# Expert rows spread over partitions by a permuted constant, and the last products among the expert turns made transposes (decoder step with mixture of experts, one core)

## The reference, cut to what matters

```python
def hmoe(h, w_rg, b_rg, w_re, b_re, w_g, w_u, w_d):
    g_prob = softmax(h @ w_rg + b_rg)              # 4 groups, the best one is taken
    e_logits = (h @ w_re + b_re)[the 8 experts of that group]
    top_p, top_i = top_k(softmax(e_logits), 2)     # two of its 8 experts
    weights = max(g_prob) * top_p / sum(top_p)
    expert = g_idx * 8 + top_i                     # 32 experts in all
    a = einsum('td,edf->tef', h, w_g)              # 1024 -> 256
    u = einsum('td,edf->tef', h, w_u)
    return einsum('tef,efd->td', silu(a) * u * comb[:, :, None], w_d)   # 256 -> 1024
```

```
layer 0: 47 40 35 37 40 27 33 39 23 31 37 25 28 21 34 27 33 33 32 32 38 26 30 34 28 36 32 27 30 40 33 32
layer 1: 25 39 35 28 33 27 25 22 32 28 31 40 28 32 32 17 34 31 44 49 27 42 37 32 23 44 37 32 36 30 35 33
```

## Time and profile before

| | |
|---|---|
| median of 3 runs | 1375.42 us |
| the profiled execution: its own time | 1374.61 us |
| its span, first to last instruction | 1372.7 us |
| PE busy | 1297.9 us, 95% of the span |
| DVE, ACT, POOL busy | 637.2, 332.1, 451.9 us |
| moved by DMA | 318.83 MB, mean 232 GB/s |
| mean granted clock of PE | 0.987 |
| mixture of layer 0, first gate product to last | 367 to 586 us |
| mixture of layer 1, the same | 1125 to 1348 us |

### The profile page before, as it was taken

One profiled execution on the slowest core, in us unless ns is written; L12 is line 12 of the kernel. 1 busy time (PEld: TensorE's weight loads), 2 busy tenths in 40 slices (PEclk: granted clock), 3 DMA queues, 4 the chain that ended last, 5 costly groups with the idle time before them and its releaser, 6 DMA issues. The chain is left out here.

```text
span 1372.7 us, 20982 instructions
## 1 busy us (share of the span) xinstructions
PE 1297.9 (95%) x8732; PEld 919.7 (67%) x8732; DVE 637.2 (46%) x997; ACT 332.1 (24%) x667; POOL 451.9 (33%) x385
## 2 busy tenths in 40 slices
PE   8999999999999998899999999999998989999786
PEld 6787888545566764547868867877845656766453
DVE  3577675623622221164558558558436472121114
ACT  2222322302122221240115005005005312222112
POOL 2233444101011111005876576576450111111101
PEclk9999999999899999999999999999999999999998
DMA  8366534377699999971112012013050899999996
GB/s 312 135 219 220 194 106 174 101 309 299 246 418 418 419 418 420 412 289 51 57 56 94 12 55 94 11 56 96 9 139 2 330 353 419 417 419 419 419 417 259
DMA packets 92768, 318.83 MB, mean 232 GB/s; under 512 B 32969, under 2 KB 45401, under 8 KB 66564
## 3 DMA queue, kind: packets, MB, share of 16 engines
q1 hardware_dynamic: 77956, 279.95, 52.5%
q0 software_dynamic: 13536, 33.29, 6.7%
q10 hardware_dynamic: 1184, 4.26, 0.8%
HBM read 300.19 MB, written 33.28 MB: 243 GB/s over the span
## 5 line engine op out<-in xcount | busy, mean ns | idle before, releaser
L1941 PE MATMUL ps<-slots 128*128 128x384 f32 x768 | 262.0, 495 | 0.9 <-DVE vo L2240 0.6
L1941 PEld LDWEIGHTS ps<-slots 128*128 128x128 f32 x768 | 203.0, 270 | 43.7 <-issue 3.2
L1092 PE MATMUL ps<-slots,oT 128*64 128x256 f32 x1344 | 178.4, 390 | 23.3 <-DMA slots<-in_w_up 18.6
L581 PE MATMUL ps<-xnT_a,wA 128*128 128x260 f32 (+1 forms) x768 | 173.3, 386 | 1.7 <-DVE xnT_a L791 1.4
L1092 PEld LDWEIGHTS ps<-slots,oT 128*64 128x64 f32 x1344 | 121.4, 141 | 74.2 <-issue 26.2
L581 PEld LDWEIGHTS ps<-xnT_a,wA 128*128 128x128 f32 x768 | 145.6, 191 | 27.0 <-issue 5.8
L1604 POOL DMA_INDIRECT y_rows<-ysb,idx x30 | 30.2, 1007 | 361.1 <-DVE ysb L1127 361.1
L1118 DVE TENSOR_TENSOR sg<-sg,ps 64x256 f32<-64x256 f32 x64 | 26.5, 414 | 236.2 <-ACT sg L1115 236.2
L1127 DVE COPY ysb<-ps 64x512 f32<-64x512 f32 x60 | 41.6, 694 | 82.8 <-PE ps L1110 82.8
L1115 ACT ACTIVATE sg<-ps 64x256 f32<-64x256 f32 x64 | 24.4, 381 | 227.5 <-PE ps L1092 227.5
L2178 ACT ACTIVATE slots<-slots,neg 128x128 f32<-128x128 f32 (+1 forms) x192 | 64.1, 417 | 54.8 <-DVE neg L2285 49.3
(11 more groups left out here) (311 smaller groups left out, 2129.5 us busy)
## 6 DMA issues: line engine op xcount, KB each, us to landing
slots<-in_w_gate SPq DMA_DIRECT2D x42, 1024.0 KB, 23.2
slots<-in_w_up SPq DMA_DIRECT2D x42, 1024.0 KB, 26.6
slots<-in_w_down SPq DMA_DIRECT2D x36, 1024.0 KB, 26.1
slots<-in_unit_weights_b SPq DMA_DIRECT2D x12, 1536.0 KB, 7.1
wA<-in_qkv_pairs_a SPq DMA_DIRECT2D x24, 512.0 KB, 4.4
apart<-in_w_down SPq DMA_DIRECT2D x8, 1024.0 KB, 27.8
spare<-in_w_down SPq DMA_DIRECT2D x8, 1024.0 KB, 24.5
apart<-in_w_up SPq DMA_DIRECT2D x6, 1024.0 KB, 27.9
```

Of the source, the lines that this page charges most:

```text
L581: last = nc.tensor.matmul(bank(6 + h)[:, 0:half], wA[:, m, k, :], xnT[:, k, half * h:half * h + half], start=(k == 0), stop=(k == KT - 1))
L1092: last = nc.tensor.matmul(bank(q)[lo:lo + CAP, 0:FE], x[:, k, :], wt[:, k, :], start=(k == 0), stop=(k == KT - 1))
L1941: last = nc.tensor.matmul(bank(i % 2)[:, 0:UW], xT[:, kt, cols], wB[:, g, kt, :], start=(kt == 0), stop=(kt == KT - 1))
```

## The change

The constant with which places are compared is permuted: slot s now belongs to place s // 4 + 16 * (s % 4). Put the other way round, row r of an expert now sits in slot 4 * (r % 16) + r // 16: rows 0 to 15 in slots 0, 4, 8, ..., 60, rows 16 to 31 in slots 1, 5, ..., 61, and so on. The constant keeps its size and the instructions that use it stay as they are. And the product that stood first in the turn of `xs`, and the first of the two of each expert in the turn of h, become transposes. The instructions stand at the same place in PE's order; on the other engines none is added, removed or moved.

```diff
-    put("iota64", np.broadcast_to(np.arange(CAP), (128, CAP)))
+    slot = np.arange(CAP)
+    put("iota64", np.broadcast_to(slot // 4 + 16 * (slot % 4), (128, CAP)))
...
                 def turn_half(pe, w, half, sig):
                     for i in range(HALFK):
-                        out, rows = bank(2 + half)[:, 128 * i:128 * i + 128], xs[w][:, HALFK * half + i:D:KT]
-                        if half == 0 and i == 0:
-                            last = nc.tensor.matmul(out, rows, ident, start=True, stop=True)
-                        else:
-                            last = nc.tensor.transpose(out, rows, ident)
+                        last = nc.tensor.transpose(bank(2 + half)[:, 128 * i:128 * i + 128], xs[w][:, HALFK * half + i:D:KT], ident)
...
                         out, cols = bank(6 + q)[:, CAP * f:CAP * f + CAP], h[:, q, f:FE:2]
-                        if product or f == 0:
+                        if product:
                             last = nc.tensor.matmul(out, cols, ident[0:CAP, 0:CAP], start=True, stop=True)
                         else:
                             last = nc.tensor.transpose(out, cols, ident[0:CAP, 0:CAP])
```

## The result

The changed kernel takes 1370.10 us in the median of 20 runs, the kernel before, beside it on the same chips, 1376.43 us. The ratio is 0.9949 with a 95% interval of 0.9937 to 0.9961: 7.0 us faster, 5.4 to 8.7 (the medians are 6.3 apart). Single runs scatter by several microseconds (1365.56 to 1376.64 after, 1373.53 to 1380.74 before), more than the three runs ahead of the prediction showed. Taken again (experiment 4), the ratio was 0.9927 (0.9905 to 0.9950). The profiled execution took 1366.19 us, with a span of 1364.3 us.

A forecast was written before the change was run, and what follows sets the result against it. The prediction took the DMA's fullest engine to bound each mixture. Terms of 4.7 us (layer 1 rows), 4.1 (layer 0 rows) and 0.8 (layer 0 start) summed to 9.6 us, giving 1366 us, range 1363 to 1371.5.

The forecast's parts named there:

- The bound and the mechanism: Both mixtures: the DMA engine with most rows works without pause and sets the last weight landing; spreading rows gains 8.8 us.
- (a): Gathers and scatters: four neighbouring partitions per engine, again after 32; layer 1 spread 13.5 us before, fullest 160 to 130 rows.
- The size of the term: Fewer rows on the fullest engine, 0.157 us each: 4.7 us in layer 1 and 4.1 us in layer 0.
- up to 27 us before it runs dry: Weight queue in a mixture: a light engine may lead the fullest by this much; the lead at the end is 14 us.
- The start: First gather and first turn of a mixture: 0.8 us gained in layer 0, between 0 and 1.2; nothing in layer 1.
- The signs: Profile after: share's fall 4 us, last "up" piece 8.8 to 9.6 us earlier in layer 1, PE's pair 12.0 to 12.3 us.
- The turns: PE's transposes: 0.7 us saved per pair, at most 0.96, hidden beside the DMA in the steady part.
- The clock: Rival in the steady pairs: without the products PE's clock falls, 12 us more a layer, 1400 us; chance 0.05.
- Hidden elsewhere: Rival: all engines' bytes together set landings, or heavy engines catch up; only 0.8 us gained, 1374.6 us; chance 0.08.
- dealing (b): Gathers and scatters: eight neighbouring partitions per engine; layer 1 spread 36 us before, more than twice the fall seen.
- dealing (c): Rival for gathers and scatters: partitions dealt one by one in turn; fullest engine 232 rows, 28 us more, 1403 us; chance 0.03.
- Half of it: Rival: a scatter, PE or an engine slow by itself is late next; some 4 to 5 us gained, 1371 us; chance 0.10.

The follow-up runs named there:

- experiment 4: The changed kernel run again without any edit, against the kernel before: ratio 0.9927, 1368.53 us.
- experiment 3: The changed kernel with another slot permutation, putting each eight rows of an expert on one DMA engine, against the kernel before: ratio 1.0169, 1400.84 us.
- 2: The kernel before with only the transposes of the change, slots as before, against the kernel before: ratio 0.9973.
- 7: The kernel before with only the first turn of a mixture made of transposes, against the kernel before: ratio 0.9978.
- 9: The kernel before, unedited, against itself: ratio 1.0017.
- 10: The kernel before with one more filler product ahead of the first turn, against the kernel before: ratio 1.0029.
- 1: The kernel before with only the permuted constant, turns as before, against the kernel before: ratio 0.9941.
- experiment 5: The changed kernel with the permutation mirrored, against the kernel before: ratio 0.9937, 1368.91 us.
- experiment 11: The changed kernel without the filler product ahead of the first turn, against the kernel before: ratio 0.9940, 1369.95 us.
- 6: The changed kernel with the starting place of the rows rotated by v % 8 for pair v, against the kernel before: ratio 0.9906, 1364.38 us.
- 12: The changed kernel with starting places rotated by pair, run a second time against the kernel before: ratio 0.9911, 1365.50 us.
- 8: The changed kernel with every gather and scatter index out of bounds, so no row moves, against the kernel before: ratio 0.9688, 1335.70 us.

## Why the prediction was right

**The bound and the mechanism.** The DMA's fullest engine sets both mixtures, and the rows make it the fullest. This was the step on which all hung, and it is shown: by the fall of the share, 14 us before and about 6 after, and by experiment 3, where the order of slots alone moves the time by 32 us with the same bytes.

**The dealing.** (a) was read from the length of the fall in the earlier trace rows. Experiment 3 confirms it: half of the engines loaded, 232 rows on the fullest, 16 us a layer. The grouping by four partitions that the Trainium skill's formula gives in "DMA: Bandwidth & Descriptors", "The descriptor swizzle", thus fits an indirect transfer too, by these times. Which number each engine has stays unseen, since no row names an engine.

**The size of the term.** Here the prediction was off. "Layer 1: 30 rows x 0.157 = 4.7 us. Layer 0: 26 rows, 4.1 us." The loops shrank by 3.0 and 1.9 us (223.4 to 220.5, 220.8 to 219.0). The price is not at fault: in the loaded stretches a packet of 4096 bytes takes 0.161 us and the 4 bytes of an empty slot 0.009. What failed is the step from rows to the lag of the last engine. It took all else on the 16 engines to be equal.

The trace can tell, though no view above prints it. Each piece raises its semaphore 16 times, and I read each raise as one engine done with its part (in experiment 3 eight of them come within 2.2 us and the other eight 8 to 22 us after the first). For the last piece of each mixture, by the means of the profiles, counted by rows x 0.157 and measured (layer 0 / layer 1, us):

```
                       first to last engine          last engine behind the mean
kernels                counted        measured       counted       measured
before, 2, 7, 9, 10    14.1 / 13.5    13.4 / 13.2    6.3 / 6.6     5.0 / 5.7
after, 1, 4, 5, 11      4.2 / 3.9      6.7 / 7.1     2.2 / 1.9     3.1 / 3.3
6, 12 (rotated)         1.9 / 1.3      3.4 / 5.4     1.3 / 0.5     1.7 / 3.2
3 (packed)             36.4 / 36.4    21.1 / 22.3   18.2 / 17.9   12.1 / 13.1
8 (no rows)               0 / 0        3.6 / 3.7       0 / 0       2.0 / 2.1
```

With no rows at all the last engine is 3.6 us behind the first. Before, the rows covered this surplus; once they are spread, it shows. The lag behind the mean, which is what the change can take away, went down by 2.0 and 2.4 us where 4.1 and 4.7 were counted. The prediction had the hint: its own idle shares gave 5.6 us before, not 6.6, but it took 1.9 for what would be left, and 3.3 was left.

What the surplus is stays open. The trace has one more queue on the same engines, that of instruction loads ("q8 instruction"): in the mixtures of the changed kernel 12 and 11 packets of 16 KB, about 1.05 us each. If they fall on a few engines more than on others they could make it; no run shows that. An engine slow by itself at the end of a half is ruled out (experiment 5), and that kernel, where the first engines of the halves have the fewest rows, has the smallest lag of the five (2.2 and 2.3 us, the others 2.6 to 4.3), which speaks for a surplus nearer to the front, from one profile each.

The rotated slots are not explained in full. Their loops fell by a further 2.8 and 1.7 us, where the lag went down by 1.4 and 0.1. All 16 engines together, by their mean, finish the last piece 1.4 us sooner after the first gate product in both layers (217.3 to 215.8, 219.3 to 217.9), with the same bytes. Why is open. In experiment 3 another limit shows: the light engines lead by 21 to 26 us from the middle of the mixture on and no further, and from 1260 to 1320 the share is 0.97 to 0.99 at 385 to 395 GB/s. That is the prediction's "up to 27 us before it runs dry".

**The start.** 0.8 us were predicted for layer 0 and none for layer 1. The starts are shorter by 0.8 and 0.6 us, means of five. These means mix kernels with either form of the first turn. The kernel before itself had 8.7 (at a clock of 0.50) and 7.7 us in layer 0 and 8.0 and 7.8 in layer 1, the changed kernel 6.9 twice and 6.9 and 7.1, so the whole change is worth about 0.8 us in each. For layer 1 I had looked at the one stretch of the earlier trace rows in which the DMA was full again. It had run dry before that. The kernel before, then the changed one, at the first gather of layer 1:

```profile
1118.00:1120.00 2.00, 2.00 (x6) 0.62 (x4) 1.74 (x7) 0.00 (x0) 1.19 (x1) 1.00 0.72 299
1120.00:1122.00 2.00, 1.11 (x5) 0.59 (x4) 1.74 (x9) 0.00 (x0) 1.00 (x1) 1.00 0.58 135
1122.00:1124.00 2.00, 1.37 (x7) 0.85 (x6) 1.83 (x6) 0.00 (x0) 0.00 (x0) 1.00 0.42 133
1124.00:1126.00 2.00, 1.27 (x11) 0.82 (x11) 1.76 (x10) 1.72 (x3) 0.56 (x1) 0.94 0.93 270
```

```profile
1112.00:1114.00 2.00, 2.00 (x5) 0.81 (x5) 1.75 (x8) 0.00 (x0) 1.01 (x1) 1.00 0.87 365
1114.00:1116.00 2.00, 1.11 (x5) 0.47 (x4) 1.76 (x9) 0.00 (x0) 1.18 (x2) 1.00 0.51 148
1116.00:1118.00 2.00, 2.00 (x10) 1.09 (x10) 1.86 (x5) 0.39 (x1) 0.00 (x0) 1.00 0.78 182
1118.00:1120.00 2.00, 1.27 (x13) 0.89 (x14) 1.66 (x12) 1.98 (x3) 0.99 (x1) 1.00 0.74 270
```

In layer 1 SP waits for the first gather itself before it issues two more pieces. SP's queue, before and after:

```profile
1123.13 0.33 SPq L354 DMA_DIRECT2D gain_rows<-in_w_down  x1
```

```profile
1116.83 0.33 SPq L355 DMA_DIRECT2D gain_rows<-in_w_down  x1
```

Counted from the row table (1117.45 and 1111.87), that is 5.68 us before and 4.96 after, 0.7 us sooner. So the gather had two that waited for it, PE and SP, and I named one. The loops and starts together went down by 1.9 + 3.0 + 0.8 + 0.6 = 6.3 us, and the runs by 7.0. The 9.6 us of the sum were 2.6 too many: 3.9 too many in the term of the rows, made up in part by the start of layer 1, for which it had nothing. The forecast's own terms ended at 1369 us, and 1370.1 lies inside the range only because the range was stretched to take in the half case. The kernel before was itself 1.0 us slower over 20 runs than in the three; less 7.0 us, those three give 1368.4.

**The signs.** The fall of the share was to last 4 us and lasted some 6. The last "up" piece of layer 1 was to land 8.8 to 9.6 us earlier and landed 7.7 earlier; the last gate product of layer 0, 4 to 5, began 3.7 earlier (582.19 to 578.50). In both 1.7 us are the chance gain of the router, so 6.0 and 2.0 are the change's. PE's pair was to be 12.0 to 12.3 us and is 12.46. Only the stretch between the mixtures did as said (530.2 us before, 529.8 after, from the result rows' first issue to the next row table). Landings that come earlier by less than the rows were named a sign of "hidden"; by experiment 3 and the lags above they mean a smaller term here and no other bound.

**The turns.** 0.96 us at most and 0.7 taken for a pair; PE's pair fell by 0.46 (12.92 to 12.46). The change-over stays with whatever comes first: the four turns of h still take 0.62 us, 0.15 each, not 0.11. That they hide under the DMA in the steady part held: the loops of experiments 2 and 7 are those of the kernel before.

**The rivals.** The clock: it did fall more often in the steady pairs. The kernel before had no low stretch between 380 and 580 in its profile, the changed one had two of 3.4 us, and three between 1249 and 1287. One of them stretched a half pair of gate products from 3.70 to 5.38 us:

```profile
1248.49 5.38 PE ps L1089 x32
```

PE waits for weights there anyway, and experiment 11, with a fall on the first gate products, was no slower. With the same turns of transposes the falls come and go with the waits for weights: between 380 and 580 the kernel without rows (waits short) had none and the packed one (waits long) seven. The rule of the Trainium skill in "TensorE: Matmul & The Clock Gate", "PE-mode transpose", is neither proved nor refuted: longer waits for weights explain the falls as well. "Hidden elsewhere" and dealing (b) are refuted by experiment 3, and dealing (c) already by the result (1370 us, not 1403). "Half of it", 1371, is 1 us from the first median, and by the loops it is a good description of the row term alone. One of the causes it named, an engine slow by itself, is near what the run without rows shows: work that is unequal without any row. That the forecast was closer in the sum is in part luck, since the start of layer 1 made up for some of the row term.

## What to carry to other kernels

Where a stretch is bound by DMA, look at how the busy share falls at its end: a slow fall says that the engines carry unequal loads, and its length is about the surplus of the fullest. Find out what of it is left without the part you mean to spread (3.6 us here) before you price the rest. Rows at the front of a tile meet few engines, in any gather with unfilled slots; a permuted index constant spreads them at no cost, and the starting slot should change from transfer to transfer as well. For differences under 0.3%, run the old kernel against itself first.

## What was not expected of the hardware

An indirect transfer whose rows lie badly costs the whole stream beside it: the same 1040 rows a layer, in another order of slots, changed the kernel from 1364 to 1401 us. And removing all rows saved 17 to 18 us a layer, a little less than the mean engine's share (118 x 0.157 = 18.5), though the fullest engine had 130: without rows the engines are still up to 3.6 us apart.
